# Scan of a two-layer decoder trunk: VectorE operands moved from SBUF to PSUM

## The chip, the cores and the metric

The kernel runs on one core of one Trainium2 chip. The metric is the time on the device of one execution, in microseconds (us). TensorE is the matrix engine, VectorE, ScalarE and GpSimd do elementwise work; SBUF is the large on-chip memory, PSUM the small one of eight banks that TensorE writes. VectorE and ScalarE reach both, GpSimd SBUF alone.

## The reference

One inference step of two layers. Each layer is a SwiGLU feed-forward part, a mixer, and a second feed-forward part, all with RMSNorm. T = 336 tokens: 8 running sequences of 8 tokens, 16 meta tokens, a prompt of 256. The mixer, cut to what matters:

```python
full = jnp.concatenate([conv0, xbc], axis=1)
xbc = jax.nn.silu(depthwise_causal_conv(full, conv_w, conv_b))     # 4 taps, 24 tiles of 128 channels
new_conv = full[:, -3:]
dt = jax.nn.softplus(dt_raw + dt_bias);  a_neg = -jnp.exp(a_log)
# ssd_scan, per chunk (80, 128 and 128 tokens) and head (32 of 64 channels)
acum = jnp.cumsum(dt * a_neg);  lmat = jnp.exp(causal(acum_i - acum_j))
xdt = x * dt
y_intra = (cb * lmat) @ xdt                                         # cb = C B^T
cs = B^T @ (xdt * exp(acum_end - acum));  state = state * chunk_decay + cs
y = y_intra + (C @ prev_state) * exp(acum) + d_skip * x
y = rmsnorm(y * silu(z)) ;  ssd_out = y @ w_ssd_branch
```

The new states, the last three rows before the convolution and the pooling rows are outputs as well.

## The kernel before

Activations stand with channels on the 128 partitions and tokens in the free dimension. Every weight product is a *unit*: 8 tiles of 128x128 weights from one 512 KB transfer. Weights and activations are split in a high and a low part, and TensorE makes three matmuls of 336 columns per tile (lines 1013, 1016, 1017). ScalarE makes the high part of the weights (`whi`, line 430), GpSimd the low part (`wlo`, line 355: `wraw - whi`, two operands in SBUF, 1024 columns). Two units are kept ahead.

The engines' programs are written by hand, in order, and meet at semaphores only. A layer has these stages: feed-forward; the **convolution stage**, in which the 8 tiles of B and C and the first of x go through `conv` (line 731); the **scan**, 16 steps of one x tile (two heads) each; pooling and gates; output; feed-forward. PSUM has four banks `gb` for weight products and four `kb` for the rest.

`conv` on VectorE scales the raw product by `rpre` into `xp` (lines 737, 738), copies the last rows to `cso` for the output (740, 741), makes the first tap's product (744) and three sums (747) in `cv`. A drain stands before each sum. ScalarE applies silu to `cv` (`silu_xbc`, lines 495, 496) and raises `xbc_done`; line 743 makes VectorE wait for that before `cv` is written again. In the convolution stage the banks rotate, `from_bc(c)` uses bank (1 + c) % 4.

A scan step t (`ssd_step`, once for each engine) is, on TensorE: the x unit of tile t + 1 into bank 1; the chunk states (line 1126); the products with the masked matrix (1134); the logarithms for t + 1 (`log_l`) into banks `gb[2]`, `gb[3]`; the z unit into bank 0 with the products from the sample states between its matmuls (1147); the products from the chained states (1156), which raise `y_full`; the update of the sample states (1162); and, after `y_read`, the transposes of tile t + 1 (1110). On VectorE: `conv` of tile t + 1; the state chain `pst`, `pfin` (787, 792), which raises `p_done`; `times_l` (768, 769); the gate input (806); the y chain (810, 812, 814, 817); `times_dt` (776, 779); the new states (825, 826), which raise `so_done`; the squares' sum (829) and the low part of y (830). Line 1126 waits for `so_done` of the step before. ScalarE does the exponents, silu of the tile and of the gate, and issues the state transfers; GpSimd decays the sample states (line 392, operands in SBUF) between two `wlo`.

A few lines that the text speaks of:

```python
l4 = lx[:, :].rearrange("p (c h i) -> p c h i", c=2, h=2)
dve.tensor_tensor(l4, l4, rep(cb[:, g, n0:T]...), ALU.mult)                       # 768, times_l
dve.tensor_tensor(t_b[:, 1, :], gb[Z_BANK][:, 0:T], rpre[:, :], ALU.mult)          # 806
dve.tensor_tensor(t_a[:, 0, :], kb[1][:, 0:T], eab[:, q, :], ALU.mult)             # 810
dve.tensor_tensor(t_a[:, 1, :], kb[0][:, 0:T], t_a[:, 0, :], ALU.add)              # 812, y_read
dve.scalar_tensor_tensor(t_a[:, 2, :], xs[:, q, :], D, t_a[:, 1, :], mult, add)    # 814
dve.tensor_tensor(t_a[:, 3, :], t_a[:, 2, :], t_b[:, 0, :], ALU.mult)              # 817
```

## Time and profile before

| | us |
|---|---|
| median of 3 runs | 2289.95 |
| lowest and highest run | 2285.34, 2296.04 |
| span of the profiled execution | 2279.0 |
| TensorE, VectorE, ScalarE, GpSimd busy | 2087.2, 1095.6, 937.1, 1248.3 |

The profile is one execution; its span runs from the first to the last instruction, and it has no other time of its own, so it is set beside the median of the runs, which is 10.95 us longer. In its rows, PE is TensorE, PEld its weight loads, DVE VectorE, ACT ScalarE, POOL GpSimd; L747 is line 747 of the kernel. A row of the timeline has the start and the length in us, engine, line, instruction, output<-inputs, shapes, and in brackets the idle time before it with the instruction that ended it. `sq` and `fo` are also the memory of `lx` and `cb`, `tail` that of `so`, `xdt`, `xdec`, `dt`, and `t_b` that of `xs`. `q` after an engine's name is its sequencer.

### The profile page before, as it was taken

How to read it: one execution, taken by the hardware profiler on the slowest of the kernel's cores; microseconds unless marked ns; L12 is line 12 of the kernel's file. 1: busy time of each engine (PE TensorE's matmuls, PEld its weight loads, DVE VectorE, ACT ScalarE, POOL GpSimd, SP SyncE). 2: the span in 40 equal slices, each digit the busy share in tenths (PEclk: the TensorE clock that was granted, in tenths of full speed). 3: DMA queues.
4: the chain of work that ended last, by engine and by line, in shares of the span. 5: the costliest groups of instructions: out<-in, count | busy, mean ns of one | idle time of the engine just before them, and what ended most of it. 6: DMA issues, size and time to landing. Idle time of an engine off the chain costs nothing.

```text
span 2279.0 us, 40931 instructions
## 1 busy us (share of the span) xinstructions
PE 2087.2 (92%) x13546; PEld 2026.9 (89%) x13546; DVE 1095.6 (48%) x2040; ACT 937.1 (41%) x1357; POOL 1248.3 (55%) x555
## 2 busy tenths in 40 slices
PE   6999878999989998999889998699998999989997
PEld 6999877888889997999879998688888999979997
DVE  3221277888944525221242213778888445252212
ACT  4343344444533434333343333444444334343432
POOL 5666642333356665666656676333333566656675
PEclk9999998999999999999999999889999999999998
DMA  4445422333344443444424453223333444434443
GB/s 172 138 144 157 138 67 84 128 118 121 116 150 139 139 143 97 146 139 148 141 91 141 147 156 115 76 97 115 115 115 128 146 139 142 144 99 141 138 156 108
DMA packets 86338, 292.38 MB, mean 128 GB/s; under 512 B 15728, under 2 KB 15728, under 8 KB 86256
## 3 DMA queue, kind: packets, MB, share of 16 engines
q1 hardware_dynamic: 68544, 249.13, 34.6%
q10 hardware_dynamic: 17712, 42.22, 5.3%
q8 instruction: 44, 0.72, 0.1%
...
HBM read 269.29 MB, written 22.02 MB: 128 GB/s over the span
## 4 chain that ended last, share of the span: by engine, by line
PE 64%; DVE 17%; DVEq 10%; issue 5%; POOL 1%; ACT 1%; DMA 1%; ACTq 0%; POOLq 0%; SPq 0%
PE gb L1013 20%; PE gb L1017 19%; PE gb L1016 19%; DVE cv L747 6%; DVEq L746 2%; DVE t_a L814 2%; DVEq L704 2%; DVEq L832 1%; POOL wlo L355 1%; DVE alo L691 1%; DVEq L777 1%; DVEq L811 1%; PE gb L1065 1%; DVE t_a L699 1%; DVE t_a L812 1%
## 5 line engine op out<-in xcount | busy, mean ns | idle before, releaser
L355 POOL TENSOR_TENSOR wlo<-wraw,whi 128x1024 fp32r<-128x1024 f32 x474 | 1141.7, 2409 | 952.3 <-ACT whi L430 933.2
L1013 PE MATMUL gb<-ahi,whi 128*128 128x336 f32 x2256 | 750.6, 333 | 23.9 <-POOL wlo L355 14.6
L1017 PE MATMUL gb<-ahi,wlo 128*128 128x336 f32 x2256 | 722.5, 320 | 0.0
L1016 PE MATMUL gb<-alo,whi 128*128 128x336 f32 x2256 | 721.9, 320 | 0.0
L430 ACT ACTIVATE whi<-wraw 128x1024 fp32r<-128x1024 f32 x474 | 494.1, 1050 | 188.9 <-PE gb L1013 116.5
L1013 PEld LDWEIGHTS gb<-ahi,whi 128*128 128x128 f32 x2256 | 433.3, 192 | 36.0 <-POOL wlo L355 27.3
L1016 PEld LDWEIGHTS gb<-alo,whi 128*128 128x128 f32 x2256 | 433.3, 192 | 0.0
L1017 PEld LDWEIGHTS gb<-ahi,wlo 128*128 128x128 f32 x2256 | 430.6, 191 | 0.0
L1013 PE MATMUL gb<-bhi,whi 128*128 128x336 f32 x1248 | 395.4, 317 | 5.0 <-DVE blo L967 5.0
L1016 PE MATMUL gb<-blo,whi 128*128 128x336 f32 x1248 | 393.4, 315 | 0.0
L1017 PE MATMUL gb<-bhi,wlo 128*128 128x336 f32 x1248 | 393.1, 315 | 0.0
L713 DVE TENSOR_TENSOR t_a<-gb,rpre 128x336 f32<-128x336 f32 x176 | 88.6, 507 | 337.9 <-PE gb L1017 336.3
L1013 PEld LDWEIGHTS gb<-bhi,whi 128*128 128x128 f32 x1248 | 234.8, 188 | 5.6 <-issue 5.6
L1016 PEld LDWEIGHTS gb<-blo,whi 128*128 128x128 f32 x1248 | 235.3, 189 | 0.0
L1017 PEld LDWEIGHTS gb<-bhi,wlo 128*128 128x128 f32 x1248 | 235.0, 188 | 0.0
L726 DVE COPY fo<-gb 128x336 f32 x48 | 24.4, 508 | 294.0 <-PE gb L1017 294.0
L747 DVE SCALAR_TENSOR_TENSOR cv<-xp,par,cv 128x360 f32<-128x360 f32 x144 | 147.3, 1023 | 29.5 <-issue 29.5
L474 ACT ACTIVATE bhi<-t_b 128x336 f32 (+1 forms) x88 | 42.7, 485 | 249.8 <-DVE t_b L716 249.8
L1065 PE MATMUL gb<-ahi,whi 128*128 128x336 f32 x192 | 68.3, 356 | 52.2 <-DVE alo L691 49.8
L487 ACT ACTIVATE sq<-fo 128x336 f32 x48 | 23.3, 486 | 224.9 <-DVE fo L726 224.9
L495 ACT ACT_TABLE_LOAD x38 | 48.8, 1283 | 136.4 <-DVE cv L747 135.8
L470 ACT ACTIVATE t_b<-t_a 128x336 f32<-128x336 f32 x88 | 42.7, 486 | 119.7 <-DVE t_a L713 119.7
...
## 6 DMA issues: line engine op xcount, KB each, us to landing
...
ssm_o<-tail ACTq DMA_DIRECT2D x32, 576.0 KB, 3.7
...
```

Source lines behind the costliest of these rows:

```text
L355: pool.tensor_tensor(wlo[:, s, :], wraw[:, s, :], whi[:, s, :].bitcast(F32), ALU.subtract).then_inc(w_lo, 1)
L430: act.activation(whi[:, slot, :], wraw[:, slot, :], ACT.Copy).then_inc(w_hi, 1)
L495: act.activation(seqs(dst[:, 0:SAMPLE], STEPS), seqs(cv[:, 0:CP], CSTRIDE)[:, :, 0:STEPS], ACT.Silu, bias=bias)
L704: dve.drain()
L713: dve.tensor_tensor(t_a[:, r, :], gb[r][:, 0:T], rpre[:, :], ALU.mult).then_inc(g_out, 1)
L746: dve.drain()
L747: ins = dve.scalar_tensor_tensor(cv[:, :], xp[:, k:k + n], pcol(L, G_CW + CONV_K * c + k), cv[:, :], ALU.mult, ALU.add)
L814: dve.scalar_tensor_tensor(t_a[:, 2, :], xs[:, q, :], pcol(L, G_D + t), t_a[:, 1, :], ALU.mult, ALU.add)
L1013: ins = pe.matmul(gb[bank][:, 0:T], whi[:, slot, w], xh, start=first and j == 0, stop=False)
L1016: pe.matmul(gb[bank][:, 0:T], whi[:, slot, w], xl, start=False, stop=False)
L1017: ins = pe.matmul(gb[bank][:, 0:T], wlo[:, slot, w], xh, start=False, stop=last and j == tiles - 1)
L1065: ins = pe.matmul(gb[s][:, 0:T], whi[:, s, w], ahi[:, j, :], start=j == 0, stop=False)
```

## The change

VectorE instructions of the scan that had both operands in SBUF get one in PSUM, where one is to be had:

- The convolution sums are made in the bank that held the raw product (`cv` is now `gb[bank]`), and the tile `cv` is gone. The rows for the output are made from the raw product again, ahead of `xp`, and raise `cso_done` there. VectorE's wait of line 743 is gone; TensorE instead waits for `xbc_done` before it writes a bank whose sums ScalarE reads.
- ScalarE writes the exponents in place in `gb[2]` and `gb[3]`, the decay per channel first; `times_l` reads them there and writes `lx`, `lx0`.
- The scaled z, its silu and y times gate stay in bank 0. TensorE waits for `b_done` of the step before the z unit overwrites it.
- y from the states is scaled in place in `kb[1]`; the sum with D x follows at once, and the sum with `kb[0]`, which raises `y_read`, comes third.
- `times_dt` takes both products from PSUM with a table `dtd` = dt x decay, made once per layer; the drain between them goes.
- The last chained state goes straight into `so`; the copy from `pfin` goes, and VectorE waits for `so_free` before the `pst` copy.

```diff
         xp = sb("xp", [P, CW])
-        cv = sb("cv", [P, CW - HIST])
         cst = sb("cst", [P, NXBC, SEQS * HIST])
...
         st = sb("st", [P, SEQS * P])
-        pfin = sb("pfin", [P, P])
         eab = sb("eab", [P, 2, T])
...
         bcur = c.take(3, P)
+        dtd = c.take(3, N_HEADS)
         c = Carve(tail[0][:, :])
...
-            def silu_xbc(L, c, dst, side):
+            def silu_xbc(L, c, dst, side, bank):
+                cv = gb[bank][:, 0:CW - HIST]
...
-            def exp_l(L, t):
+            def exp_l(L, t, q):
                 act.wait_ge(l_full, L * KI + t + 1)
-                act.activation(lx, gb[2][:, :], ACT.Exp)
+                act.activation(gb[2][:, :], gb[2][:, :], ACT.Exp)
                 n0 = CHUNKS[0][1]
-                act.activation(lx0[0:n0, :, :].rearrange("p a b -> p (a b)"), gb[3][0:n0, 0:2 * n0], ACT.Exp).then_inc(l_exp, 1)
-
-            def exp_e(q):
-
-                act.activation(eab[:, q, :], gb[3][:, 2 * CHUNKS[0][1]:2 * CHUNKS[0][1] + T], ACT.Exp).then_inc(e_exp, 1)
+                act.activation(eab[:, q, :], gb[3][:, 2 * n0:2 * n0 + T], ACT.Exp).then_inc(e_exp, 1)
+                act.activation(gb[3][0:n0, 0:2 * n0], gb[3][0:n0, 0:2 * n0], ACT.Exp).then_inc(l_exp, 1)
...
                     ahead(L, "ssd", 1 + 2 * q, 2 * t - 2 * q)
-                    exp_l(L, t + 1)
-                    exp_e(1 - q)
-                    silu_xbc(L, 2 * N_GROUPS + t + 1, xs[:, 1 - q, :], 1 - q)
+                    exp_l(L, t + 1, 1 - q)
+                    silu_xbc(L, 2 * N_GROUPS + t + 1, xs[:, 1 - q, :], 1 - q, XS_BANK)
                 z = z_at(t, last)
...
                 act.wait_ge(g_out, L * N_G + M0["ssd"] + z + 1 + RING)
-                act.activation(t_b[:, 0, :], t_b[:, 1, :], ACT.Silu).then_inc(gate_done, 1)
+                zb = gb[Z_BANK][:, 0:T]
+                act.activation(zb, zb, ACT.Silu).then_inc(gate_done, 1)
                 act.wait_ge(val_in, L * N_VAL + V_Y + t + 1)
-                act.activation(bhi[:, t, :], t_a[:, 3, :], ACT.Copy, scale=par[:, L, bass.ds(G_SSD + t, 1)]).then_inc(hi_done, 1)
-                act.activation(sq[:, 0, :], t_a[:, 3, :], ACT.Square).then_inc(sq_done, 1)
+                act.activation(bhi[:, t, :], zb, ACT.Copy, scale=par[:, L, bass.ds(G_SSD + t, 1)]).then_inc(hi_done, 1)
+                act.activation(sq[:, 0, :], zb, ACT.Square).then_inc(sq_done, 1)
                 if not last:
...
                         act.activation(dec[:, :], kb[3][:, 0:2 * DK + SEQS * N_HEADS], ACT.Exp).then_inc(dec_done, 1)
-                        exp_l(L, 0)
-                        exp_e(0)
+                        exp_l(L, 0, 0)
                         evict_cb(L, 0)
                         evict_cb(L, 1)
-                    silu_xbc(L, c, bc[:, c, :], c % 2)
+                    silu_xbc(L, c, bc[:, c, :], c % 2, (1 + c) % RING)
                     if c >= N_GROUPS:
...
                 evict_cb(L, 2)
-                silu_xbc(L, 2 * N_GROUPS, xs[:, 0, :], 0)
+                silu_xbc(L, 2 * N_GROUPS, xs[:, 0, :], 0, XS_BANK)
                 evict_cb(L, 3)
...
                 h3 = seqs(xp[:, 0:CP], CSTRIDE)
+                raw = gb[bank][:, 0:T]
+                last = STEPS - HIST
                 dve.tensor_copy(h3[:, :, 0:HIST], seqs(cst[:, c, :], HIST))
-                dve.tensor_tensor(h3[:, :, HIST:CSTRIDE], seqs(gb[bank][:, 0:SAMPLE], STEPS), seqs(rpre[:, 0:SAMPLE], STEPS), ALU.mult)
-                dve.tensor_tensor(xp[:, CP + HIST:CW], gb[bank][:, SAMPLE:T], rpre[:, SAMPLE:T], ALU.mult).then_inc(g_out, 1)
+                dve.tensor_tensor(seqs(cso[:, side, 0:SEQS * HIST], HIST), seqs(raw[:, 0:SAMPLE], STEPS)[:, :, last:STEPS],
+                                  seqs(rpre[:, 0:SAMPLE], STEPS)[:, :, last:STEPS], ALU.mult)
+                dve.tensor_tensor(cso[:, side, SEQS * HIST:CKEEP], raw[:, T - HIST:T], rpre[:, T - HIST:T], ALU.mult).then_inc(cso_done, 1)
+                dve.tensor_tensor(h3[:, :, HIST:CSTRIDE], seqs(raw[:, 0:SAMPLE], STEPS), seqs(rpre[:, 0:SAMPLE], STEPS), ALU.mult)
+                dve.tensor_tensor(xp[:, CP + HIST:CW], raw[:, SAMPLE:T], rpre[:, SAMPLE:T], ALU.mult).then_inc(g_out, 1)
                 dve.drain()
-                dve.tensor_copy(seqs(cso[:, side, 0:SEQS * HIST], HIST), h3[:, :, STEPS:CSTRIDE])
-                dve.tensor_copy(cso[:, side, SEQS * HIST:CKEEP], xp[:, CW - HIST:CW]).then_inc(cso_done, 1)
                 n = CW - HIST
-                dve.wait_ge(xbc_done, L * NXBC + c + 1)
-                dve.tensor_scalar(cv[:, :], xp[:, 0:n], pcol(L, G_CW + CONV_K * c), None, ALU.mult)
+                cv = gb[bank][:, 0:n]
+                dve.tensor_scalar(cv, xp[:, 0:n], pcol(L, G_CW + CONV_K * c), None, ALU.mult)
                 for k in range(1, CONV_K):
                     dve.drain()
-                    ins = dve.scalar_tensor_tensor(cv[:, :], xp[:, k:k + n], pcol(L, G_CW + CONV_K * c + k), cv[:, :], ALU.mult, ALU.add)
+                    ins = dve.scalar_tensor_tensor(cv, xp[:, k:k + n], pcol(L, G_CW + CONV_K * c + k), cv, ALU.mult, ALU.add)
                 ins.then_inc(cv_in, 1)
...
                 n0 = CHUNKS[0][1]
-                l4 = lx[:, :].rearrange("p (c h i) -> p c h i", c=2, h=2)
-                dve.tensor_tensor(l4, l4, rep(cb[:, g, n0:T].rearrange("p (c i) -> p c i", c=2), 2, 2), ALU.mult)
-                dve.tensor_tensor(lx0[0:n0, :, :], lx0[0:n0, :, :], rep(cb[0:n0, g, 0:n0], 2, 1), ALU.mult).then_inc(m_done, 1)
+                l4, e4 = (v[:, :].rearrange("p (c h i) -> p c h i", c=2, h=2) for v in (lx, gb[2]))
+                dve.tensor_tensor(l4, e4, rep(cb[:, g, n0:T].rearrange("p (c i) -> p c i", c=2), 2, 2), ALU.mult)
+                dve.tensor_tensor(lx0[0:n0, :, :], gb[3][0:n0, 0:2 * n0].rearrange("p (h i) -> p h i", h=2),
+                                  rep(cb[0:n0, g, 0:n0], 2, 1), ALU.mult).then_inc(m_done, 1)
...
                 dve.tensor_tensor(v[0], xt, heads(dt[:, :, bass.ds(2 * t, 2)]), ALU.mult)
-                dve.drain()
-                de = dec[:, 0:DK].rearrange("p (c h) -> p c h", c=3)[:, :, bass.ds(2 * t, 2)]
-                dve.tensor_tensor(v[1], v[0], heads(de), ALU.mult).then_inc(xd_done, 1)
+                dve.tensor_tensor(v[1], xt, heads(dtd[:, :, bass.ds(2 * t, 2)]), ALU.mult).then_inc(xd_done, 1)
...
                 dve.wait_ge(cs_full, kt + 1)
+                dve.wait_ge(so_free, 16 * kt + 16)
                 dve.tensor_copy(pst[:, 0, :], kb[3][:, 0:P])
                 dve.drain()
-                for c, dst in ((1, pst[:, 1, :]), (2, pfin[:, :])):
+                for c, dst in ((1, pst[:, 1, :]), (2, so[:, SEQS * P:SO])):
                     for h in range(2):
...
                 dve.wait_ge(g_full, L * N_G + z + 1)
-                dve.tensor_tensor(t_b[:, 1, :], gb[Z_BANK][:, 0:T], rpre[:, :], ALU.mult).then_inc(g_out, 1)
+                zb, yi = gb[Z_BANK][:, 0:T], kb[1][:, 0:T]
+                dve.tensor_tensor(zb, zb, rpre[:, :], ALU.mult).then_inc(g_out, 1)
...
                 dve.wait_ge(y_full, kt + 1)
-                dve.tensor_tensor(t_a[:, 0, :], kb[1][:, 0:T], eab[:, q, :], ALU.mult)
+                dve.tensor_tensor(yi, yi, eab[:, q, :], ALU.mult)
+                dve.drain()
+                dve.scalar_tensor_tensor(t_a[:, 0, :], xs[:, q, :], pcol(L, G_D + t), yi, ALU.mult, ALU.add)
                 dve.drain()
...
                 dve.drain()
-                dve.scalar_tensor_tensor(t_a[:, 2, :], xs[:, q, :], pcol(L, G_D + t), t_a[:, 1, :], ALU.mult, ALU.add)
-                dve.drain()
                 dve.wait_ge(gate_done, L * N_GATE + KF + t + 1)
-                dve.tensor_tensor(t_a[:, 3, :], t_a[:, 2, :], t_b[:, 0, :], ALU.mult).then_inc(val_in, 1)
+                dve.tensor_tensor(zb, zb, t_a[:, 1, :], ALU.mult).then_inc(val_in, 1)
                 if not last:
...
                     cols = slice(b * 4 * P, (b + 1) * 4 * P)
-                    dve.tensor_tensor(so[:, cols], so[:, cols], kb[2 + b][:, :], ALU.add)
-                dve.tensor_copy(so[:, SEQS * P:SO], pfin[:, :]).then_inc(so_done, 1)
+                    ins = dve.tensor_tensor(so[:, cols], so[:, cols], kb[2 + b][:, :], ALU.add)
+                ins.then_inc(so_done, 1)
                 dve.wait_ge(hi_done, L * N_HI + H_Y + t + 1)
...
                 dve.tensor_tensor(acc[:, :], acc[:, :], sq[:, 0, :], ALU.add)
-                dve.scalar_tensor_tensor(blo[:, t, :], t_a[:, 3, :], pcol(L, G_SSD + t), bhi[:, t, :].bitcast(F32),
+                dve.scalar_tensor_tensor(blo[:, t, :], zb, pcol(L, G_SSD + t), bhi[:, t, :].bitcast(F32),
                                          ALU.mult, ALU.subtract).then_inc(b_done, 1)
...
                 dve.wait_ge(cb_free, (L + 1) * N_GROUPS)
+                dve.tensor_tensor(dtd[:, :, :], dt[:, :, :], dec[:, 0:DK].rearrange("p (c h) -> p c h", c=3), ALU.mult)
+                dve.drain()
                 times_dt(L, 0)
...
                     pe.wait_ge(g_out, L * N_G + M0["ssd"] + 2 * t + 1 + RING)
+                    pe.wait_ge(xbc_done, L * NXBC + 2 * N_GROUPS + t + 2)
                     unit(L, U0["ssd"] + 2 * t + 1, slot_of("ssd", 2 * q + 1), XS_BANK, ahi, alo, 0, True, True)
...
                     pe.wait_ge(g_out, L * N_G + M0["ssd"] + 2 * t + 1 + RING)
+                pe.wait_ge(b_done, L * N_B + KF + t)
                 pe.wait_ge(st_landed, 16 * (L * KI + t) + 16)
...
                 def from_bc(c):
+                    if c >= RING:
+                        pe.wait_ge(xbc_done, L * NXBC + c - RING + 2)
                     from_a(L, U0["bc"] + c, slot_of("bc", c), M0["bc"] + c, (1 + c) % RING)
...
                 b_token_major(2)
+                pe.wait_ge(xbc_done, L * NXBC + 2 * N_GROUPS - RING + 2)
                 from_a(L, U0["ssd"], slot_of("ssd", 0), M0["ssd"], XS_BANK)
```

What that makes of the order on VectorE, in the first scan step of the loop, from the history copy of `conv` on. Before:

```order
L736 COPY xp<-cst 128x8x3
L737 TENSOR_TENSOR xp<-gb,rpre 128x8x8
L738 TENSOR_TENSOR xp<-gb,rpre 128x272
L740 COPY cso<-xp 128x24
L741 COPY cso<-xp 128x3
L743 ISA
L744 ISA [waits xbc_tile_ready]
L744 TENSOR_SCALAR cv<-xp,par 128x360
L747 ISA
```

Now:

```order
L734 COPY xp<-cst 128x8x3
L735 TENSOR_TENSOR cso<-gb,rpre 128x24
L737 TENSOR_TENSOR cso<-gb,rpre 128x3
L738 TENSOR_TENSOR xp<-gb,rpre 128x8x8
L739 TENSOR_TENSOR xp<-gb,rpre 128x272
L743 ISA
L743 TENSOR_SCALAR gb<-xp,par 128x360
L746 ISA
L746 SCALAR_TENSOR_TENSOR gb<-xp,par,gb 128x360
```

The two `cso` instructions moved ahead of `xp` and read `gb`; the wait for `xbc_tile_ready` (that is `xbc_done`) is gone; the product and the sums write `gb`.

The y chain of the same step, on VectorE (`y_products_ready` is `y_full`, `gate_ready` is `gate_done`). Before:

```order
L806 TENSOR_TENSOR t_b<-gb,rpre 128x336 [waits gemm_bank_full]
L810 TENSOR_TENSOR t_a<-kb,eab 128x336 [waits y_products_ready,decay_per_channel_ready]
L812 TENSOR_TENSOR t_a<-kb,t_a 128x336
L814 ISA
L814 SCALAR_TENSOR_TENSOR t_a<-t_b,par,t_a 128x336
L816 ISA
L817 TENSOR_TENSOR t_a<-t_a,t_b 128x336 [waits gate_ready]
```

Now:

```order
L806 TENSOR_TENSOR gb<-gb,rpre 128x336 [waits gemm_bank_full]
L810 TENSOR_TENSOR kb<-kb,eab 128x336 [waits y_products_ready,decay_per_channel_ready]
L812 ISA
L812 SCALAR_TENSOR_TENSOR t_a<-t_b,par,kb 128x336
L814 TENSOR_TENSOR t_a<-kb,t_a 128x336
L816 ISA
L817 TENSOR_TENSOR gb<-gb,t_a 128x336 [waits gate_ready]
```

The sum with D x stands second and reads `kb`; the sum of the two y parts, which releases TensorE's transposes, stands third.

TensorE in the same step, between `log_l` and the z unit. Before:

```order
L1102 MATMUL gb<-maskr,identr 80x160
L1104 MATMUL gb<-rx,halfr 128x336 x2
L1141 ISA
L1009 ISA [waits states_landed]
L1013 MATMUL gb<-ahi,whi 128x336 [waits w_lo_ready]
```

Now:

```order
L1104 MATMUL gb<-maskr,identr 80x160
L1106 MATMUL gb<-rx,halfr 128x336 x2
L1144 REGISTER_ALU
L1145 ISA [waits b_tile_ready]
L1011 ISA [waits states_landed]
L1015 MATMUL gb<-ahi,whi 128x336 [waits w_lo_ready]
```

One wait is added, for `b_tile_ready` (`b_done`).

## Rows read from the trace of the kernel before

**Rows 1.** The page: busy us (share); the chain by engine; a transfer, us to landing.
```profile
PE 2087.2 (92%) x13546; PEld 2026.9 (89%) x13546; DVE 1095.6 (48%) x2040; ACT 937.1 (41%) x1357; POOL 1248.3 (55%) x555
...
PE 64%; DVE 17%; DVEq 10%; issue 5%; POOL 1%; ACT 1%; DMA 1%; ACTq 0%; POOLq 0%; SPq 0%
...
ssm_o<-tail ACTq DMA_DIRECT2D x32, 576.0 KB, 3.7
```

**Rows 2.** Windows: convolution stage of layer 0, and 13 scan steps of each layer.
```profile
core 0: us, PE busy (x) PEld busy (x) DVE busy (x) ACT busy (x) POOL busy (x), PEclk, DMA share, GB/s
298.39:358.86 60.47, 40.14 (x226) 37.64 (x226) 47.49 (x103) 28.05 (x49) 17.34 (x7) 0.80 0.26 81
...
388.57:621.77 233.20, 215.34 (x1497) 197.31 (x1496) 202.94 (x371) 113.62 (x182) 86.59 (x39) 0.97 0.37 122
1520.76:1756.77 236.01, 219.50 (x1497) 201.85 (x1496) 200.94 (x371) 113.60 (x182) 86.61 (x39) 0.95 0.36 120
```

**Rows 3.** Timeline of one scan step, VectorE and GpSimd: start, length, instruction.
```profile
562.24 2.37 POOL L355 TENSOR_TENSOR wlo<-wraw,whi 128x1024 fp32r<-128x1024 f32 x1 [5.48 <-ACT whi L430]
...
562.52 2.12 DVE L740 COPY cso<-xp 128x24 f32<-128x24 f32 x1
...
565.05 1.92 POOL L392 TENSOR_TENSOR tail<-st,dec 128x1024 f32<-128x1024 f32 x1 [0.44 <-POOL wlo L355]
...
565.26 2.09 DVE L747 SCALAR_TENSOR_TENSOR cv<-xp,par,cv 128x360 f32<-128x360 f32 x1 [0.24 <-issue]
...
567.59 0.59 DVE L747 SCALAR_TENSOR_TENSOR cv<-xp,par,cv 128x360 f32<-128x360 f32 x1 [0.24 <-issue]
...
572.27 2.37 POOL L355 TENSOR_TENSOR wlo<-wraw,whi 128x1024 fp32r<-128x1024 f32 x1 [5.30 <-ACT whi L430]
...
573.30 1.70 DVE L814 SCALAR_TENSOR_TENSOR t_a<-t_b,par,t_a 128x336 f32<-128x336 f32 x1 [0.27 <-issue]
```

**Rows 4.** Timeline of the same step, TensorE.
```profile
560.46 1.10 PE L1126 MATMUL kb<-tail,tail 16*128 16x128 f32 x6 [0.90 <-DVE tail L826]
...
570.58 0.71 PE L1156 MATMUL kb<-bc,fo 128*128 x4 [0.94 <-DVE pfin L792]
...
571.22 2.05 PE L1162 MATMUL kb<-tail,fo 64*128 64x128 f32 x16
...
578.29 0.46 PE L1126 MATMUL kb<-tail,tail 16*128 16x128 f32 x2 [0.67 <-issue]
```

**Rows 5.** Two source lines over the whole run: shortest/median/longest ns.
```profile
L713 DVE TENSOR_TENSOR t_a<-gb,rpre x176: 497/508/510, 35.8 to 2181.3; 128x336 f32<-128x336 f32 x176
...
L716 DVE TENSOR_TENSOR t_b<-t_a,t_b x88: 507/509/1622, 37.0 to 2182.0; 128x336 f32<-128x336 f32 x88
```

**Rows 6.** Timeline of the convolution stage, layer 0: one blocked sum.
```profile
320.87 2.55 POOL L355 TENSOR_TENSOR wlo<-wraw,whi 128x1024 fp32r<-128x1024 f32 x1 [4.36 <-ACT whi L430]
...
321.39 2.42 DVE L747 SCALAR_TENSOR_TENSOR cv<-xp,par,cv 128x360 f32<-128x360 f32 x1 [0.18 <-issue]
```

**Rows 7.** Timeline of the end of the convolution stage, layer 0.
```profile
354.88 0.41 DVE L744 TENSOR_SCALAR cv<-xp,par 128x360 f32<-128x360 f32 x1 [3.96 <-ACT bc L496]
...
355.16 1.65 PE L1218 MATMUL kb<-bc 128*128 128x80 f32 x6 [1.91 <-ACT tail L541]
...
358.86 0.90 PE L1110 MATMUL kb<-con,t_b 128*128 128x128 f32 x3 [2.05 <-ACT fo L545]
```

**Rows 8.** Timeline of the first scan step: the y chain, nothing blocked.
```profile
374.18 2.05 PE L1162 MATMUL kb<-tail,fo 64*128 64x128 f32 x16
374.35 0.51 DVE L810 TENSOR_TENSOR t_a<-kb,eab 128x336 f32<-128x336 f32 x1 [0.45 <-PE kb L1156]
...
375.71 0.57 DVE L814 SCALAR_TENSOR_TENSOR t_a<-t_b,par,t_a 128x336 f32<-128x336 f32 x1 [0.26 <-issue]
```

**Rows 9.** Timeline of TensorE before the last step of layer 0.
```profile
631.00 1.92 PE L1126 MATMUL kb<-tail,tail 16*128 16x128 f32 x6 [4.62 <-DVE tail L826]
```

**Rows 10.** Timeline of VectorE at the first convolution of layer 0.
```profile
298.39 1.83 DVE L736 COPY xp<-cst 128x24 f32<-128x24 f32 x1 [0.30 <-issue]
```

## The prediction

> **What bounds the kernel now.** I read the page first. TensorE is busy 92% of the span and VectorE 48%, yet the chain that ended last gives VectorE and its queue 27% [rows 1]. So VectorE holds the end in some stages only, and the shares of the whole do not tell what this change is worth. The windows show where: 47.49 of 60.47 us busy in the convolution stage and 202.94 of 233.20 in thirteen scan steps of layer 0 [rows 2]. A step takes 233.20/13 = 17.94 us, in layer 1 236.01/13 = 18.15.
>
> Then the timeline of one step. VectorE works without a break there, and three of its instructions take far longer than their size asks for: the copy of 24 columns 2.12 us, one sum of 360 columns 2.09 where its twin takes 0.59, and the y sum 1.70 [rows 3], which takes 0.57 when free [rows 8]. Each lies on a GpSimd instruction: 562.24 to 564.61, 565.05 to 566.97 and 572.27 to 574.64 [rows 3], and VectorE's one ends just behind it. All three read SBUF only. Line 713, with one operand in PSUM, never took over 510 ns in 176 executions, line 716, with two in SBUF, up to 1622 [rows 5]. So the blocks come from what the instruction reads, and a PSUM operand avoids them, at least as a source.
>
> TensorE waits twice in the step: 0.94 us for `pfin` before line 1156, and 0.67 to 0.90 for the new states before line 1126 [rows 4]. That is all VectorE can give back per step while TensorE has its own work.
>
> **The scan step, VectorE's side.** Removed: the block on the staged copy, 2.12 less some 0.2 (my estimate for 24 columns, from 0.59 for 360); on the sum, 2.09 - 0.59 = 1.50; on the y sum, 1.70 - 0.57 = 1.13. That is 4.55 us. The `pfin` copy and the drain inside `times_dt` go too, some 0.3 together. Added: the first product of a convolution, now 0.41 [rows 7] from SBUF to SBUF, writes PSUM. No row has a VectorE write to PSUM. Below, it stays 0.41; above, I take the 0.59 of a sum of the same 360 columns [rows 3], and use 0.59, the nearer row in size and shape. For the other in-place writes I take today's durations, with the same row as reason; the dearer case is a rival. VectorE's work per step becomes 17.94 - 4.55 - 0.3 + 0.2 = 13.3 us.
>
> **The scan step, TensorE's side.** Its work does not shrink: 215.34/13 = 16.56 us busy per step in layer 0 and 219.50/13 = 16.88 in layer 1, at a granted clock of 0.97 and 0.95 [rows 2]. So TensorE bounds the step next, and 3 us of VectorE's gain per step is hidden. Busy time counts the modelled end of a matmul before each of the two gaps, some 0.3 us too much. Against that stands the new y chain. In the first step, where nothing is blocked, the three y instructions begin at 374.35 and end at 375.71 + 0.57 = 376.28 [rows 8]; today `y_read` rises after two of them, now after all three. TensorE covers that with line 1162, which ends at 374.18 + 2.05 = 376.23 [rows 8]. So the wait is 0.05 us and a semaphore's hop, some 0.2 with it. I take 16.5 and 16.8 us: 13 x (17.94 - 16.5) + 13 x (18.15 - 16.8) = 18.7 + 17.6 = 36 us.
>
> The other waits that the step gains. Before the z unit TensorE waits for `b_done` of the step before; that is VectorE's line 830, which ends about when line 1126 starts, and line 1134 and `log_l` stand between: nothing. Before the `pst` copy VectorE waits for the stored states: issued right after `so_done`, landing in 3.7 us [rows 1], while a convolution of some 4 us (four long instructions of 0.59, drains and copies) stands in front of the wait. A late transfer delays `p_done`, which TensorE wants only behind the z unit: 0, and up to 1 us in a few steps. Behind that wait are queued the state chain, `times_l` and the y chain, so it would matter if the transfer took 7 us each time. ScalarE does the same exponents in another order and in place: the product that wants them comes a step later: nothing. TensorE's wait on the convolution bank repeats one that the transposes already make.
>
> **The last step** has no convolution, so TensorE stood 4.62 us for VectorE's states [rows 9]. That chain loses the 1.13, the copy and the drain: 1.5 us, 3 for both layers. In the first step TensorE is the bound already: nothing. The new table `dtd`, one short product and a drain per layer, stands before the first `times_dt`, which waits for TensorE's transposes of 0.90 us [rows 7] at that moment: nothing.
>
> **The convolution stage.** Here VectorE is the bound. One sum in each of six convolutions is blocked, as the one of 2.42 us that lies on GpSimd's 320.87 to 323.42 [rows 6]: 6 x (2.42 - 0.59) = 11.0 us. Dearer first products before the last rows are ready: 7 x 0.18 = 1.3. At the end VectorE waited 3.96 us for ScalarE before the last convolution [rows 7]; with the sums in their own bank that wait is gone, and the last tile comes early. Next late is the product of line 1218, done at 355.16 + 1.65 = 356.81, and its eviction of 336 columns by ScalarE, which I put at the 0.51 of line 810 [rows 8]: about 357.3 against 358.86 [rows 7], 1.5 us. TensorE now may write a bank only when ScalarE has read the sums, one convolution later than today, but four banks keep it two or more tiles ahead. Some 0.7 us goes where GpSimd catches the history copy that stays in SBUF. So 11.0 - 1.3 + 1.5 - 0.7 = 10.5 per layer, 21 for both; bounds 0 and 15 per layer.
>
> **Sum.** 36 + 3 + 21 = 60 us off a span of 2279.0: 2219. The median of the runs is 2289.95, 10.95 above the profiled span, and I keep that distance: **2230 us**. A difference under 0.5%, 11.4 us, is about what measuring this kernel cannot tell from none.
>
> A rule speaks against the change. The Trainium skill (VectorE: DVE Perf Modes, section on the TRN2 errata) gives VectorE a fixed part of 58 cycles from SBUF and 120 from PSUM, 65 ns more per instruction. The rows show 508 against 509 ns at the median [rows 5], so I charge nothing. By the rule, an estimate from that page, four instructions in 18 convolutions and three in the y chain of 28 steps would give back about 10 us, and the time would be 2240.
>
> **Rivals.**
> Better, 2213: TensorE's clock stays up. The window of thirteen steps ran at 0.97 and 0.95 [rows 2]; with fewer gaps the 4% come back, 26 x 0.65 = 17 us. Against it: neither gap is long. Chance 0.09.
>
> The block moves, 2252: the history copy of line 736 and the `acc` sum still read SBUF alone, and line 736 was caught once for 1.83 us [rows 10]. Six catches per layer in the convolution stage return 22 us; in the scan 3 us of slack hide them. For it: GpSimd is as busy as before and its instructions now find other victims. The Trainium skill (SBUF — State Buffer, Who interferes with whom) says that such a copy, in a two-port mode, contends as well, and that an instruction with one SBUF input does not. Chance 0.14.
>
> TensorE waits elsewhere, 2246: y chain, stored states or PSUM writes leave 0.6 us per step, 16 us. Chance 0.12.
>
> No gain, 2290: the blocks do not depend on what is read, or writing PSUM is blocked too. Rows 5 speak against the first. Chance 0.04.
>
> Slower, 2318: an instruction that reads and writes one PSUM bank runs at a fraction of the rate. No row excludes it. With x us more per in-place instruction, the convolution stages lose 54x; the scan has six in a step, and from x = 0.53 VectorE (13.3 + 6x) is the bound again, 28 x 6x. The gain of 60 is used up at x = 0.67, a sum of 1.26 us in place of 0.59; at 0.8 the kernel loses 28 us. Line 713's 508 ns for 336 columns makes this unlikely. Chance 0.04.
>
> **How the numbers follow.** The forecast holds 0.57, in 2217 to 2243: steps of 16.2 to 16.9, stage gains of 7 to 13 per layer. The range must leave out at most 0.2, so it takes in both middle rivals and most of the better one: 2211 to 2262. Faster by over 0.5% are all but the last two cases: 0.92; same 0.04; slower 0.04.
>
> **What would show it.** Right: sums of the convolution near 0.59 us at the median and at the longest, the y sum near 0.57, a first product near 0.59, a step of 16.5 us in which TensorE has no gap over 0.3 us and VectorE idles about 3, a convolution stage near 50 us, and an unchanged rest. Wrong: sums that stay above 1 us, long history copies, TensorE waiting before line 1156's successor or its transposes, or a step over 17.3 us.

## The result and the profile after

| | median of runs, us | lowest, highest | ratio to before [95%] |
|---|---|---|---|
| before | 2287.64 | 2283.06, 2296.04 | |
| changed | 2210.48 | 2207.79, 2213.59 | 0.9648 [0.9623, 0.9674] |

The change makes the kernel 3.5% faster. The forecast was 2230 us with a range from 2211: direction and mechanism hold, the size was underestimated, and the median lies half a microsecond below the range. The profiled execution has a span of 2211.8 us and an own time of 2213.59, the longest of the four.

The page after: VectorE and its queue fell from 27% of the chain [rows 1] to 11%, and a sum takes 598 ns in the mean where it took 1023.

```profile
PE 2081.6 (94%) x13546; PEld 2023.1 (91%) x13546; DVE 952.4 (43%) x2010; ACT 932.1 (42%) x1357; POOL 1245.7 (56%) x555
...
PE 83%; DVE 8%; DVEq 3%; issue 2%; POOL 1%; ACT 1%; DMA 1%; ACTq 0%; POOLq 0%; SPq 0%
...
L746 DVE SCALAR_TENSOR_TENSOR gb<-xp,par,gb 128x360 f32<-128x360 f32 x144 | 86.1, 598 | 29.4 <-issue 29.4
...
ssm_o<-tail ACTq DMA_DIRECT2D x32, 576.0 KB, 3.2
```

Windows after: the convolution stage of layer 0, from VectorE's first history copy to TensorE's transposes as in [rows 2], thirteen scan steps from chunk states to chunk states, and the stretch from the last chunk states to the last `acc` sum (lines 1129 to 829), these two in both layers.

```profile
core 0: us, PE busy (x) PEld busy (x) DVE busy (x) ACT busy (x) POOL busy (x), PEclk, DMA share, GB/s
298.68:346.19 47.51, 38.57 (x226) 36.95 (x226) 37.49 (x102) 27.28 (x49) 16.12 (x7) 0.86 0.34 103
368.15:579.04 210.89, 208.21 (x1496) 190.67 (x1496) 146.25 (x357) 112.43 (x183) 86.47 (x39) 1.00 0.41 135
593.76:614.04 20.28, 20.28 (x85) 19.05 (x86) 5.81 (x14) 2.37 (x4) 4.24 (x2) 0.50 0.20 70
1467.23:1678.17 210.94, 208.25 (x1496) 190.69 (x1495) 146.34 (x357) 112.41 (x183) 86.47 (x39) 1.00 0.41 135
1692.89:1713.17 20.28, 20.28 (x85) 19.05 (x86) 5.80 (x14) 2.37 (x4) 4.24 (x2) 0.50 0.20 73
```

The windows of before that answer to them (the convolution stage is in [rows 2]): thirteen steps of layer 0 between the same matmuls, and the last stretch of both layers.

```profile
380.35:613.64 233.29, 215.43 (x1497) 197.40 (x1496) 202.50 (x370) 113.61 (x182) 86.59 (x39) 0.97 0.36 121
631.00:645.12 14.12, 14.12 (x93) 13.10 (x94) 5.84 (x16) 2.49 (x4) 4.25 (x2) 0.85 0.29 105
1766.00:1780.84 14.84, 14.84 (x93) 13.82 (x94) 5.84 (x16) 2.49 (x4) 4.25 (x2) 0.80 0.28 103
```

So a step fell from 233.29/13 = 17.95 us to 16.22, at a clock of 1.00 in place of 0.97, and the convolution stage from 60.47 to 47.51. But the last stretch became 6.16 and 5.44 us longer, at a granted clock of 0.50, the lower level of 1.2 GHz.

Timeline of one scan step after, VectorE, GpSimd and TensorE together:

```profile
514.81 0.18 DVE L734 COPY xp<-cst 128x24 f32 x1 [0.71 <-PE gb L1019]
...
515.10 2.36 POOL L354 TENSOR_TENSOR wlo<-wraw,whi 128x1024 fp32r<-128x1024 f32 x1 [6.53 <-ACT whi L429]
...
515.90 0.59 DVE L743 TENSOR_SCALAR gb<-xp,par 128x360 f32<-128x360 f32 x1 [0.28 <-issue]
...
516.73 0.60 DVE L746 SCALAR_TENSOR_TENSOR gb<-xp,par,gb 128x360 f32<-128x360 f32 x1 [0.24 <-issue]
...
517.90 1.92 POOL L391 TENSOR_TENSOR tail<-st,dec 128x1024 f32<-128x1024 f32 x1 [0.44 <-POOL wlo L354]
...
518.41 0.60 DVE L746 SCALAR_TENSOR_TENSOR gb<-xp,par,gb 128x360 f32<-128x360 f32 x1 [0.24 <-issue]
...
522.19 2.36 POOL L354 TENSOR_TENSOR wlo<-wraw,whi 128x1024 fp32r<-128x1024 f32 x1 [2.37 <-ACT whi L429]
...
523.42 0.52 DVE L806 TENSOR_TENSOR gb<-gb,rpre 128x336 f32<-128x336 f32 x1 [2.10 <-PE gb L1019]
...
524.20 2.05 PE L1166 MATMUL kb<-tail,fo 64*128 64x128 f32 x16
...
525.78 0.51 DVE L814 TENSOR_TENSOR t_a<-kb,t_a 128x336 f32<-128x336 f32 x1
...
526.42 0.54 PE L1112 MATMUL kb<-con,t_b 128*128 128x128 f32 x3 [0.17 <-DVE t_a L814]
```

GpSimd's three instructions are as long as before [rows 3]. The sums at 516.73 and 518.41 lie fully or partly under them and take 0.60 us. The first product (line 743) rose from 0.41 to 0.59, as assumed. New is a gap of 0.17 us on TensorE before its transposes (line 1112), which wait for the third y instruction (line 814). VectorE idles 2.10 us before line 806: it is not the bound.

What still reads and writes SBUF alone is still held, where GpSimd meets it. Timeline after, at the first convolution of layer 0:

```profile
298.09 2.39 POOL L354 TENSOR_TENSOR wlo<-wraw,whi 128x1024 fp32r<-128x1024 f32 x1 [0.24 <-POOL wlo L354]
...
298.68 1.84 DVE L734 COPY xp<-cst 128x24 f32<-128x24 f32 x1 [0.30 <-issue]
```

That is the same 1.8 us as before [rows 10].

The two profiled spans, piece by piece, both layers together (the convolution stage of layer 1 runs from 1429.81 to 1490.21 before and from 1397.77 to 1445.26 after, its thirteen steps from 1512.56 to 1748.63 before):

| piece | forecast | measured |
|---|---|---|
| thirteen scan steps | -36 | 22.40 + 25.13 = -47.5 |
| last scan step, up to its chunk states | -3 | 2.64 + 2.65 = -5.3 |
| convolution stage | -21 | 12.96 + 12.91 = -25.9 |
| stretch behind the last chunk states | 0 | 6.16 + 5.44 = +11.6 |
| everything else | 0 | -0.1 |
| span | -60 | -67.2 |

### The profile page after: what moved, and what is told of

Read it like the earlier page. It is cut to its first block, busy times and chain, and to the rows that moved or that the text cites. A ratio compares the mean times of both kernels' runs of the same rounds, so it can differ in the third digit from the quotient of the medians.

```text
span 2211.8 us, 40913 instructions
## 1 busy us (share of the span) xinstructions
PE 2081.6 (94%) x13546; PEld 2023.1 (91%) x13546; DVE 952.4 (43%) x2010; ACT 932.1 (42%) x1357; POOL 1245.7 (56%) x555
## 4 chain that ended last, share of the span: by engine, by line
PE 83%; DVE 8%; DVEq 3%; issue 2%; POOL 1%; ACT 1%; DMA 1%; ACTq 0%; POOLq 0%; SPq 0%
PE gb L1015 25%; PE gb L1019 23%; PE gb L1018 23%; DVEq L700 2%; PE kb L1129 2%; PE kb L1151 1%; PE kb L1137 1%; DVE gb L746 1%; POOL wlo L354 1%; PE kb L1166 1%; PE gb L1067 1%; PE kb L1160 1%; PE kb L1112 1%; PE gb L1070 1%; PE gb L1071 1%
## 5 line engine op out<-in xcount | busy, mean ns | idle before, releaser
L746 DVE SCALAR_TENSOR_TENSOR gb<-xp,par,gb 128x360 f32<-128x360 f32 x144 | 86.1, 598 | 29.4 <-issue 29.4
L1151 PEld LDWEIGHTS kb<-bc,st 128*128 128x128 f32 x512 | 91.9, 197 | 0.0
```

Source lines behind the costliest of these rows:

```text
L746: ins = dve.scalar_tensor_tensor(cv, xp[:, k:k + n], pcol(L, G_CW + CONV_K * c + k), cv, ALU.mult, ALU.add)
L1151: pe.matmul(kb[1][:, c], st[:, b * P:(b + 1) * P], bc[:, cg, c], start=True, stop=True)
```

## Experiments

All medians in us, each with its ratio to runs of the kernel before on the same chip.

| label | kernel | median | ratio [95%] |
|---|---|---|---|
| after_again | the changed kernel | 2210.97 | 0.9625 [0.9603, 0.9647] |
| e1_conv | convolution part alone | 2202.71 | 0.9632 [0.9606, 0.9657] |
| e2_rest | all but the convolution part | 2255.62 | 0.9862 [0.9813, 0.9910] |
| e3_structure | table and direct write alone | 2278.89 | 0.9957 [0.9939, 0.9975] |
| e5_warm | changed, last step filled | 2204.66 | 0.9595 [0.9575, 0.9615] |
| e7_order | changed, y order of before | 2196.01 | 0.9563 [0.9541, 0.9586] |
| e10_both | both edits | 2191.85 | 0.9545 [0.9526, 0.9564] |
| e12_conv_warm | convolution part, last step filled | 2190.94 | 0.9579 [0.9562, 0.9596] |
| e8_two | changed, 2 more products a step | 2214.77 | 0.9677 [0.9658, 0.9695] |
| e9_five | changed, 5 more | 2326.28 | 1.0157 [1.0135, 1.0179] |
| e13_five_filled | 5 more, TensorE's wait filled | 2272.26 | 0.9914 [0.9887, 0.9941] |
| e14_before_filled | before, TensorE's wait filled | 2290.65 | 1.0002 [0.9985, 1.0019] |

**Which part of the change it is.** Three kernels divide it. e1 takes the convolution's PSUM sums, the staged rows and the waits that they need into the kernel before:

```diff
-                ins = dve.scalar_tensor_tensor(cv[:, :], xp[:, k:k + n], ..., cv[:, :], ALU.mult, ALU.add)
+                cv = gb[bank][:, 0:n]
...
+                ins = dve.scalar_tensor_tensor(cv, xp[:, k:k + n], ..., cv, ALU.mult, ALU.add)
```

> Only the convolution part of the change: the convolution's sums in the tile's own PSUM bank, the staged rows taken from the projection's bank. Theory (VectorE lost its time where GpSimd's subtraction held an instruction that reads SBUF alone, and TensorE bounds the step once VectorE has 2 us to spare): two of the three held instructions of a step are freed, 3.6 of 4.75 us, so VectorE needs about 14.4 us and TensorE's 16.2 bound the step; the y sum stays held (longest 1.7 us) and may leave TensorE waiting up to 0.6 us per step. 2212 to 2232 us; convolution stage 47.5 us as with the whole change, step 16.2 to 16.9. Rival (the whole change matters, as fewer copies, drains and instructions add up evenly): about half of the 77 us, 2245 to 2255, step about 17.1.

e2 is the changed kernel without these lines.

> The whole change without its convolution part: exponents, gate and y in PSUM, the table and the direct write of the final state stay; convolution sums back in SBUF. Theory of the held instructions: the convolution stage is as long as before (60.4 us a layer, +26 for both), the step keeps its held copy and its held sum, 3.6 us, so VectorE needs 13.2 + 3.6 = 16.8 us and bounds it again: 2210 + 26 + 26 x 0.3 to 0.8 = 2244 to 2258 us. Rival (evenly spread): 2245 to 2255 as well, but with sums that are not held; the rows of the sum (mean above 0.9 us, longest above 2) tell them apart.

e3 has of the change only `dtd` and the final state written straight into `so`.

> Only the parts that save an instruction and move no operand to PSUM: the table of the two factors and the final state written at once into the outgoing tile. Theory of the held instructions: 0.3 to 0.5 us per step on the bound engine and about 0.5 in each last step: 8 to 15 us, 2272 to 2280. Rival (instructions and drains saved are the gain): most of the 77 us, under 2240.

The convolution part alone gives 86 us against before, where the whole change gave 77 and, in after_again, 86: it carries the whole gain. Its median of 2202.71 is below both expected ranges and 8 us below the changed kernel's two (2210.48, 2210.97), but the ratios do not tell the two kernels apart; the rows of a step below do. e2 gives 33 and e3 10, both within what the theory of the held instructions had. In e2 the sums are held as before; its group in the page:

```profile
L743 DVE SCALAR_TENSOR_TENSOR cv<-xp,par,cv 128x360 f32<-128x360 f32 x144 | 149.3, 1037 | 29.4 <-issue 29.4
```

The dropped `pfin` copy, drain and product are worth 10 us, so it is not the fewer copies and drains that gain. The parts do not add (86 + 33 against 77 or 86), since each frees VectorE, and once the step is 2 us shorter (17.95 to about 16) TensorE bounds it. And part of the rest costs something. TensorE's timeline in a step of e1, and the window of thirteen steps:

```profile
519.81 2.05 PE L1166 MATMUL kb<-tail,fo 64*128 64x128 f32 x16
521.78 0.55 PE L1113 MATMUL kb<-con,t_b 128*128 128x128 f32 x3
...
367.98:573.37 205.39, 205.39 (x1496) 190.37 (x1496) 147.94 (x371) 114.16 (x183) 86.69 (x39) 1.00 0.43 139
```

No gap before the transposes, TensorE busy in all of the window, and a step of 15.80 us, 205.39/13, in place of 16.22. The wait of up to 0.6 us that was expected behind the held y sum did not come.

**What GpSimd must do to hold VectorE.** The kernel before, with GpSimd's subtraction cut to one column, and a memset or a copy for the other 1023. Neither makes the low parts of the weights:

```diff
-                pool.tensor_tensor(wlo[:, s, :], wraw[:, s, :], whi[:, s, :].bitcast(F32), ALU.subtract).then_inc(w_lo, 1)
+                pool.tensor_tensor(wlo[:, s, 0:1], wraw[:, s, 0:1], whi[:, s, 0:1].bitcast(F32), ALU.subtract)
+                pool.memset(wlo[:, s, 1:].bitcast(F32), 0.0).then_inc(w_lo, 1)
```

> The kernel before, in which GpSimd's subtraction of 1024 columns is replaced by one of a single column and a memset of the other 1023, which reads nothing; the low parts of the weights are left out by it. Theory 1 (VectorE is held while GpSimd has both its reads running): no sum over 0.65 us, no copy of line 740 over 0.6, step near 16.5, time 2205 to 2235. Theory 2 (any GpSimd instruction that uses SBUF holds it, reads or writes): sums still held, to the length of the memset (0.9 to 2 us), time above 2250.

> As the run with the memset, but GpSimd copies 1023 columns of the raw weights: one read and one write. In the convolution stage, where GpSimd does nothing else: theory 1 (a sum with two operands in SBUF is held only by a GpSimd instruction with two reads): no sum over 0.65 us there, while the copies of line 741 or 737 are held where they meet it. Theory 2 (one read of GpSimd is enough): sums under a GpSimd copy take 1 us and more.

One run each: 2183.42 us with the memset, 2192.89 with the copy, the first below the expected 2205. A step takes 15.84 us in both where 16.5 was expected, which is 28 x 0.66 = 18 us. GpSimd is also done sooner in every other stage, so the rows are the measure here and not the times. With the memset, in the convolution stage:

```profile
302.15 0.95 POOL L356 MEMSET wlo<- 128x1023 f32 x1
...
302.19 0.59 DVE L748 SCALAR_TENSOR_TENSOR cv<-xp,par,cv 128x360 f32<-128x360 f32 x1 [0.18 <-issue]
```

The sum with two operands in SBUF runs its normal 0.59 us under an instruction of GpSimd that only writes; none of the 27 sums of this stage takes over 0.65. The stage, from the first history copy at 295.12 to the transposes at 343.26, takes 48.14 us in layer 0, against 60.47 before and 47.51 in the changed kernel. Here VectorE's wait of line 743 stands as before. So in layer 0 the gain of the stage comes with the held instructions, and the removal of that wait, a rival, is worth little. In layer 1 this stage takes 42.66, so something else gains there as well. In a scan step of the same kernel:

```profile
429.79 0.95 POOL L356 MEMSET wlo<- 128x1023 f32 x1
...
429.91 0.86 DVE L741 COPY cso<-xp 128x24 f32<-128x24 f32 x1
...
431.19 1.92 POOL L393 TENSOR_TENSOR tail<-st,dec 128x1024 f32<-128x1024 f32 x1 [0.44 <-POOL wlo L356]
...
431.21 2.28 DVE L748 SCALAR_TENSOR_TENSOR cv<-xp,par,cv 128x360 f32<-128x360 f32 x1 [0.24 <-issue]
```

Here the small copy is held by the memset (0.86 us), which theory 1 excluded, while theory 2 would have held the sums as well; and the sum by the state decay of line 393 (2.28), which still reads two operands; so "no sum over 0.65" failed in the scan, where a second instruction of GpSimd had been overlooked. With a copy on GpSimd, in the convolution stage:

```profile
302.31 1.03 POOL L356 CAST wlo<-wraw 128x1023 fp32r<-128x1023 f32 x1
...
302.36 1.37 DVE L748 SCALAR_TENSOR_TENSOR cv<-xp,par,cv 128x360 f32<-128x360 f32 x1 [0.18 <-issue]
```

One read of GpSimd is enough: 1.37 us here and 1.23 to 1.37 in six of the stage's 27 sums, so theory 2 of that run holds. The six take 7.61 us where 6 x 0.59 = 3.54 would do, and the stage takes 52.21 us in layer 0, 4.07 more than with the memset: the same difference. Sums collide with GpSimd's reads, copies already with its writes. The Trainium skill (SBUF — State Buffer, Who interferes with whom) says both: two SBUF inputs contend with a GpSimd instruction that reads, not with one that only writes, while copies in a two-port mode contend in general. The four pairs of rows agree; that the copy of 24 columns runs in such a mode no run here shows.

**The half clock behind the last step, and the y order.** The changed kernel again, and three variants:

> The changed kernel once more, so that the next three stand beside it on one chip. 2207 to 2214 us; if the length of the half-clock stretch behind the last scan step (20.3 us in both layers of its first profile) is a matter of how an execution falls, this profile shows another length in at least one layer and its own time moves with it; if it belongs to the kernel, both layers show 20 us again.

e5 fills TensorE's idle time in the last scan step:

```diff
+                if last:
+                    for _ in range(14):
+                        pe.matmul(gb[XS_BANK][:, 0:T], identr[:, :], ahi[:, 0, :], start=True, stop=True)
                 pe.wait_ge(xd_done, kt + 1)
```

> The changed kernel with 14 matmuls of no use (128 x 336, into the free tile bank) on TensorE in each last scan step, where it idled 2.40 us. Clock theory: the granted clock stays 1.00 there, the stretch from the last chunk states to the last acc sum falls from 20.3 to about 12 us in each layer; at most 16 us less, and where other executions have shorter half-clock stretches, 6 to 10 us less in the median: 2198 to 2205. Rival (the low clock does not come from the idle time in front of it): the stretch stays 20 us and the time within 2 us of the changed kernel's.

e7 raises `y_read` behind two instructions again and keeps the PSUM operands:

```diff
-                dve.tensor_tensor(yi, yi, eab[:, q, :], ALU.mult)
+                dve.tensor_tensor(t_a[:, 0, :], yi, eab[:, q, :], ALU.mult)
                 dve.drain()
-                dve.scalar_tensor_tensor(t_a[:, 0, :], xs[:, q, :], pcol(L, G_D + t), yi, ALU.mult, ALU.add)
+                dve.tensor_tensor(yi, kb[0][:, 0:T], t_a[:, 0, :], ALU.add).then_inc(y_read, 1)
                 dve.drain()
-                dve.tensor_tensor(t_a[:, 1, :], kb[0][:, 0:T], t_a[:, 0, :], ALU.add).then_inc(y_read, 1)
+                dve.scalar_tensor_tensor(t_a[:, 1, :], xs[:, q, :], pcol(L, G_D + t), yi, ALU.mult, ALU.add)
```

> The changed kernel with the order of before in the y chain: y_read rises behind two instructions again, the third one (D times x) comes after it. Theory (the gap of 0.17 us before the transposes and their slower start is the three-instruction chain, and accounts for the 16.17 us of a step against 15.80 with the convolution part alone): the gap goes, a step takes 15.80 us, 28 x 0.37 = 10 us less: 2198 to 2203. Rival (only the 0.17 us count): 4 to 5 us less. Second rival (another part of the change, such as TensorE's wait for the gate's tile, makes the step longer): no change, 2208 to 2213.

e10 has both edits.

> Both edits. If the two costs are separate, their gains add: 2188 to 2196 us, and the runs lie closer together than those of the changed kernel, with a mean granted clock of 0.975 or more in all of them. If the half-clock stretch only moves elsewhere, it equals the run with the y order alone, 2198 to 2203.

The last stretches of the changed kernel's second profile, with the same idle time of 2.40 us in front of both:

```profile
593.68:607.29 13.61, 13.61 (x92) 12.69 (x93) 5.71 (x15) 2.38 (x4) 4.26 (x2) 0.87 0.29 104
1688.51:1708.80 20.29, 20.29 (x85) 19.06 (x86) 5.81 (x15) 2.37 (x4) 4.23 (x2) 0.50 0.20 71
```

In one layer the low clock ends early (13.61 us), in the other it lasts (20.29). Other kernels with the same 2.40 us lie between: 18.19 and 14.57 us in the two layers of e8, 17.73 and 15.47 in e13. With the idle time filled:

```profile
595.33:607.43 12.10, 12.10 (x92) 11.45 (x92) 5.72 (x15) 2.38 (x4) 4.26 (x2) 1.00 0.32 121
1690.83:1702.93 12.10, 12.10 (x92) 11.45 (x93) 5.71 (x15) 2.38 (x4) 4.24 (x2) 1.00 0.32 114
```

12.10 us at full clock in both layers, and 6.3 us off the median, at the small end of what was expected. So the idle time brings the low clock; how long it stays differs from one stretch to the next within one execution. e7, thirteen steps and its two last stretches:

```profile
367.43:572.83 205.40, 205.40 (x1497) 190.44 (x1496) 144.82 (x357) 112.48 (x183) 86.40 (x39) 1.00 0.41 139
587.42:606.91 19.49, 19.49 (x85) 18.45 (x86) 5.81 (x15) 2.37 (x4) 4.24 (x2) 0.52 0.20 77
1679.94:1693.55 13.61, 13.61 (x92) 12.70 (x93) 5.71 (x15) 2.37 (x4) 4.25 (x2) 0.87 0.30 110
```

Steps of 15.80 us, TensorE busy without a break: the theory, with 15 us off the median where 10 were expected. The gap was 0.17 us, the step lost 0.42; the steps in which the group changes, 16.3 to 16.6 us in the changed kernel, are 15.8 here too. TensorE's timeline shows where an ordinary step, 16.16 us in the changed kernel, lost 0.36. First the changed kernel's x unit behind the transposes shown above, then the same place in e7:

```profile
526.84 0.41 PE L1015 MATMUL gb<-ahi,whi 128*128 128x336 f32 x1
```
```profile
519.26 2.05 PE L1166 MATMUL kb<-tail,fo 64*128 64x128 f32 x16
521.24 0.55 PE L1112 MATMUL kb<-con,t_b 128*128 128x128 f32 x3
521.54 0.40 PE L1015 MATMUL gb<-ahi,whi 128*128 128x336 f32 x1
```

From line 1166 to the transposes it is 2.22 us in the changed kernel and 1.98 in e7, and from there to the x unit 0.42 and 0.30. So 0.24 is lost in front of the transposes and 0.12 behind them; in e7 the transposes begin before the modelled end of line 1166. Together, 19 us off (2210.97 to 2191.85); five runs lie within 2.1 us, 2191.15 to 2193.28. Their mean clock was 0.972 to 0.975, where 0.975 or more was expected.

**Is anything left of the rest of the change?**

> The convolution part alone, with 16 idle-filling matmuls in each last scan step. Theory (in the scan everything but the convolution part only shortens an engine that already waits, so it is worth nothing, and the y order costs): equal to the run with both edits on the whole change, 2190 to 2195 us, step 15.80, stretch behind the last chunk states 12.1 us in both layers. Rival (exponents, gate, y, table and direct write bring something once the clock is equal): 3 to 10 us slower than that run, 2195 to 2202.

2190.94 against 2191.85, steps of 15.80 and last stretches of 12.3 in place of 12.1. The two ran on different chips, with before at 2287.05 and 2296.77, so the ratios differ, and by them alone e10 would be 8 us ahead, which is the rival's size. The medians, the profiled spans (2186.6 and 2191.3) and the steps show no such gain: as far as they tell, exponents, gate and y in PSUM, the table and the direct write bring nothing once the sums are in PSUM. Of the versions run here that compute the reference, this one and e10 are the fastest; both beat the changed kernel.

**How much VectorE has to spare.** Products repeated in the scan's convolution:

```diff
+                for _ in range(extra):
+                    dve.tensor_scalar(cv, xp[:, 0:n], pcol(L, G_CW + CONV_K * c), None, ALU.mult)
+                    dve.drain()
                 dve.tensor_scalar(cv, xp[:, 0:n], pcol(L, G_CW + CONV_K * c), None, ALU.mult)
```

> The changed kernel with two first products more per convolution in the scan (2 x 0.83 = 1.7 us of VectorE's time per step, same result). Theory (TensorE bounds the step; VectorE idles 2.1 us before the gate's product of line 806): the idle time falls to about 0.4 us, the step stays 16.17: within 4 us of the changed kernel, 2207 to 2215. Rival (VectorE's chain is still in the bound): 27 x 1.7 = 45 us more.

> The same with five more (4.2 us per step). The idle 2.1 us before line 806 is used up and 2.0 to 2.1 us per step come out: a step of 18.2 us, 27 x 2.05 = 55 us more, 2262 to 2270. If VectorE had the 3 us of slack that the prediction gave it, 27 x 1.2 = 32 us more, 2243; if it had none, 113 us more.

Waits of VectorE before the gate's product (us in all, times, longest), the changed kernel in 372 to 583 us and e8 in 400 to 560:

```profile
DVE gb L806 <- PE gb L1019: 22.1, 13, 2.4
```
```profile
DVE gb L809 <- PE gb L1022: 3.5, 7, 0.7
```

The wait falls from 1.7 us in the mean to 0.5, and two products more cost 4 us by the medians, 4.6 us in the scan steps of the two profiles: TensorE is the bound. Five cost 115 us where 55 were expected. TensorE's waits and the window of e9:

```profile
PE kb L1163 <- DVE tail L794: 13.4, 8, 2.5
```
```profile
400.00:560.00 160.00, 145.94 (x866) 135.47 (x866) 116.08 (x248) 64.34 (x107) 49.22 (x23) 0.82 0.29 98
```

It waits 1.7 us for the state chain each time, which is about the 2 us expected, but the clock is 0.82, and a step takes 20.6 us where 18.2 were expected. e13 fills this wait:

```diff
+                for _ in range(12):
+                    pe.matmul(kb[2][:, 0:T], identr[:, :], ahi[:, 0, :], start=True, stop=True)
                 pe.wait_ge(p_done, kt + 1)
```

> The kernel with five more first products, in which TensorE waits 1.5 us per step at line 1163 for the state chain and runs its window at a clock of 0.82, plus 12 matmuls of no use (about 1.7 us) in front of that wait in every step. Clock theory (half of the 116 us is the low clock that the waits bring, not the waits): granted clock back to 0.97 or more, step 18.2 to 18.6 us in place of 20.6, 27 x 2.2 = 60 us less: 2262 to 2275. Rival (VectorE's chain alone sets the step of 20.6 us, and the low clock only fills the time): no gain, 2320 to 2340, as VectorE's work has not changed.

e14 puts 6 such matmuls into the kernel before.

> The kernel before with 6 matmuls of no use (0.85 us) ahead of TensorE's wait for the final state (line 1156, 0.75 to 0.89 us per wait). Its thirteen-step windows ran at a clock of 0.97 and 0.95, which is 7.2 and 11.3 us of TensorE's busy time above the 208.2 at 1.00. If this low clock was in the bound beside VectorE's held instructions: clock 0.99 to 1.00 in both windows and 8 to 18 us less, 2270 to 2279. If VectorE alone bounded the step before: the clock rises and the time stays, 2284 to 2292. If the filling delays TensorE more than it saves: up to 10 us slower.

The window of e13, and the thirteen steps of e14 in both layers, between the same matmuls as before:

```profile
400.00:560.00 160.00, 157.66 (x1121) 145.37 (x1121) 124.46 (x285) 75.63 (x124) 59.74 (x27) 1.00 0.37 123
```
```profile
382.14:615.58 233.44, 221.76 (x1575) 202.83 (x1574) 202.62 (x370) 113.64 (x182) 86.70 (x39) 1.00 0.37 121
1514.97:1748.15 233.18, 221.53 (x1574) 202.75 (x1574) 202.27 (x370) 113.64 (x182) 87.29 (x39) 1.00 0.37 121
```

With the same work on VectorE and more on TensorE, e13 is 54 us faster than e9, at 2272, with steps of 18.1 us, as the clock theory had it: half of the 115 us was the low clock that the waits brought. In e14 the clock rises to 1.00 in both layers. In layer 0 the thirteen steps take 233.44 us where before took 233.29, in layer 1 233.18 where it took 236.07, and the median does not move. Low clock had stretched TensorE's busy time by about 7 and 11 us there, of which 0 and 3 were in the time: VectorE's held instructions were the bound, and a slow TensorE in the scan was nearly free.

## Why the prediction was right and where it was wrong

**The cause was right.** Held instructions of VectorE, about 4.6 us per step and one sum in most convolutions, go away when one operand is in PSUM. No sum of the convolution is over 0.60 us after, the y product with D takes 0.56 where it took 1.70, and the first product 0.59 as taken. The slower rival falls: a sum in place in one bank takes 0.60 against 0.59. The 65 ns per PSUM operand that the prediction names do not appear either: line 814 of after, like line 713 of before, takes 0.51, and a product in place in one bank (lines 806, 810, 817) 0.52. The moved block (2252) is seen once in each convolution stage, 1.84 and 1.83 us as in [rows 10], not six times. The stored states land in 3.2 us, in front of their wait, except in the last step, where nothing hangs on them.

**"I take 16.5 and 16.8 us" was the step of the sum that failed.** The steps took 16.22 us. The floor came from TensorE's busy time in windows at a clock of 0.97 and 0.95. e14 shows what this clock was: a consequence of TensorE's waits, nearly free while VectorE was the bound, and gone once it was not. At 1.00, thirteen steps of layer 0 are 208.21 us busy in place of 215.43, and without the gap, in e1 and e7, TensorE's step is 15.80 us. The rival "TensorE's clock stays up" said this, with 17 us and a chance of 0.09, on the ground that "neither gap is long". It came true in the scan: 11 of its 17 us lie in the 47.5. The 0.2 us charged to the y chain was there as a gap of 0.17 but cost 0.42, by e7. The idle time of about 3 us that VectorE was to have in a step came: 0.71 us before its first copy, 2.10 before line 806 and 0.44 before line 810.

**The last steps** gained 5.3 instead of 3. Unforeseen was what the shorter idle time of 2.40 us did behind itself. In before it was 4.62 and the stretch ran at 0.85; after, at 0.50. As after_again shows 13.61 and 20.29 for the same gap, the 11.6 us of the first profile are no property of the change. Nor does a longer gap decide it: e3 has 14.36 us behind 3.83 in one layer and 20.28 behind 4.31 in the other. Timeline of TensorE there, in layer 0:

```profile
593.76 1.91 PE L1129 MATMUL kb<-tail,tail 16*128 16x128 f32 x6 [2.40 <-DVE tail L825]
...
597.24 0.65 PE L1015 MATMUL gb<-ahi,whi 128*128 128x336 f32 x1
```

A matmul that takes 0.40 at full clock takes 0.65. "The last step: 3 for both layers" took the idle time as the only cost; in this profile the clock behind it was the larger one.

**The convolution stage** gave 12.9 per layer for 10.5. VectorE's busy time fell by 47.49 - 37.49 = 10.0 where the sum had 11.0 - 1.3 - 0.7 = 9.0; six sums were held in each layer, as taken, and the 0.7 for the history copy did not come. Its idle time fell from 12.98 to 10.02, 3.0 for the 1.5 that the end of the stage was given: the product of line 1218, on which the prediction let the end hang, moved forward with the rest. It had begun 3.70 us before the transposes; as line 1225 it begins at 344.64, 1.55 before them.

**"I keep that distance" failed by as much as the steps.** Of the 19.5 us between 2230 and 2210.48, 7 are in the spans (67 for 60) and 12 in the distance from span to median: 10.95 assumed, and 2210.48 - 2211.8 = -1.3 after. A run's own time is 1.8 us above its own span here (2213.59 and 2211.8), and this execution was 3.1 us above the median. By the same 1.8, before's profiled execution was one of about 2281, faster than any of its timed runs, of which the fastest took 2283.06. So the 10.95 measured how fast that one execution was, and the next profile need not share it. The mean granted clock goes with this. Before's runs beside e5 and e7 go from 2287.50 at a mean granted clock of 0.953 to 2302.38 at 0.945, and beside e1 from 2283.89 at 0.959; its profile had 0.961. The changed kernel goes from 2205.44 at 0.975 to 2213.59 at 0.964. Whether the clock is the cause of this spread is not shown. By e14 the clock of the scan steps moves before's time by 3 us at most; whether and in which other stages it does more, the runs' means don't tell.

Not settled: why the work behind a gap of 0.17 us starts another 0.12 late, and what decides how long the low clock stays.
